# Dilated attention by token parity, and new keys turned by VectorE and stored in 128-byte pieces

## The reference

```
h = rms(x); z = h @ w_in        # q, k, v of three dilated groups (4 heads of 64 each), q, k, v of a fourth mixer, two gates
for (window, dil) in ((128, 1), (512, 4), (2048, 16)):
    query t attends to keys t, t-dil, t-2*dil, ... not further back than window
    softmax of scores + mask; o_g = p @ v; lse_g = log of the softmax denominator
A = sum over the three groups of o_g, weighted by softmax of lse_g      # for the 256 prompt tokens and for the sample tokens
B = sliding-window attention with sinks
x = x + (sigmoid(g_A) * (A @ w_a) + sigmoid(g_B) * (B @ w_b)) @ w_out
outputs beside y: for every group the last `window` rows of keys and values,
   new_a1/a2/a3/b_prompt (.., tokens, 2, heads, 64) and new_.._sample (.., 8 sequences, tokens, 2, heads, 64)
```

## Time and profile before

| | |
|---|---|
| median of 3 runs | 1465.62 us (1464.95 to 1465.94) |
| profiled execution, its own time | 1465.52 us |
| its span, first to last instruction | 1463.7 us |
| granted clock of TensorE, mean | 0.997 of full |
| busy: TensorE, VectorE, ScalarE, GpSimd | 99%, 54%, 46%, 24% |
| DMA, mean over the span | 239 GB/s, 70.7% of the 16 engines' time |

### The profile page before, as it was taken

The page is one execution under the profiler, slowest core; times in us unless marked ns, Lnnn a source line. Parts: engine busy times, 40 slices in busy tenths (PEclk is TensorE's granted clock), DMA queues, the critical chain, the costliest instruction groups (busy, mean ns, idle before and its releaser), DMA issues.

```text
span 1463.7 us, 30875 instructions
## 1 busy us (share of the span) xinstructions
PE 1451.5 (99%) x11336; PEld 1413.1 (97%) x11336; DVE 794.4 (54%) x1281; ACT 669.2 (46%) x1109; POOL 349.3 (24%) x349
## 2 busy tenths in 40 slices
PE   9999999999999999999999999999999999999997
PEld 9999999999889999999999999999998899999997
DVE  5555445855545755554455554477555476555443
ACT  6444344454554544434444443445555545444442
POOL 1322212212115232220032221132121163222200
PEclk9999999999999999999999999999999999999998
DMA  8985566898764788546788846669878558884563
GB/s 309 357 287 178 167 204 203 314 335 288 247 242 137 257 327 291 181 144 198 220 314 295 293 148 182 203 199 341 297 255 284 181 185 286 315 285 144 161 195 109
DMA packets 94978, 349.79 MB, mean 239 GB/s; under 512 B 12336, under 2 KB 23984, under 8 KB 92208
## 3 DMA queue, kind: packets, MB, share of 16 engines
q1 hardware_dynamic: 94752, 348.64, 70.7%
q10 hardware_dynamic: 144, 0.03, 0.0%
HBM read 343.51 MB, written 94.37 MB: 299 GB/s over the span
## 4 chain that ended last, share of the span: by engine, by line
PE 94%; POOL 2%; DVE 1%; issue 1%; ACT 1%; DMA 1%; SPq 0%; DVEq 0%; ACTq 0%; POOLq 0%
PE ps L643 29%; PE ps L644 28%; PE ps L645 28%; PE ps L891 2%; PE ps L905 2%; POOL ma L1592 1%; PE ps L742 1%; PE ps L829 1%; PE ps L791 1%; POOL mlo L1595 0%; ACT whi L1032 0%; PE ps L752 0%; PE ps L818 0%; PE ps L796 0%; DMA x<-in_x 0%
## 5 line engine op out<-in xcount | busy, mean ns | idle before, releaser
L1254 DVE TENSOR_TENSOR wlo<-raw,whi 128x1024 fp32r<-128x1024 f32 (+2 forms) x414 | 485.4, 1173 | 375.0 <-ACT whi L1032 374.5
L643 PE MATMUL ps<-xhi,whi 128*128 128x320 f32 x2048 | 641.3, 313 | 0.9 <-DVE wlo L1254 0.5
L645 PE MATMUL ps<-xhi,wlo 128*128 128x320 f32 x2048 | 632.7, 309 | 0.0
L644 PE MATMUL ps<-xlo,whi 128*128 128x320 f32 x2048 | 632.6, 309 | 0.0
L1032 ACT ACTIVATE whi<-raw 128x1024 fp32r<-128x1024 f32 (+2 forms) x414 | 397.7, 963 | 307.0 <-PE ps L645 300.7
L643 PEld LDWEIGHTS ps<-xhi,whi 128*128 128x128 f32 x2048 | 384.5, 188 | 11.7 <-issue 9.6
L644 PEld LDWEIGHTS ps<-xlo,whi 128*128 128x128 f32 x2048 | 384.7, 188 | 0.5
L645 PEld LDWEIGHTS ps<-xhi,wlo 128*128 128x128 f32 x2048 | 384.4, 188 | 0.0
L643 PE MATMUL ps<-act_hi,whi 128*128 128x320 f32 x704 | 217.5, 309 | 0.0
L644 PE MATMUL ps<-act_lo,whi 128*128 128x320 f32 x704 | 217.5, 309 | 0.0
L645 PE MATMUL ps<-act_hi,wlo 128*128 128x320 f32 x704 | 217.5, 309 | 0.0
(11 more groups left out here) (157 smaller groups left out, 1185.3 us busy)
## 6 DMA issues: line engine op xcount, KB each, us to landing
out_new_a_sample<-in_cache_a SPq DMA_DIRECT2D x128, 510.0 KB, 5.3
raw<-in_ffn_gate SPq DMA_DIRECT2D x87, 512.0 KB, 3.7
raw<-in_ffn_up SPq DMA_DIRECT2D x87, 512.0 KB, 4.5
raw<-in_w_in SPq DMA_DIRECT2D x80, 512.0 KB, 4.9
kvc<-in_kcache SPq DMA_DIRECT2D x52, 512.0 KB, 6.9
kvc<-in_vcache SPq DMA_DIRECT2D x52, 512.0 KB, 5.3
raw<-in_ffn_down SPq DMA_DIRECT2D x64, 384.0 KB, 3.2
raw<-in_ffn_down SPq DMA_DIRECT2D x64, 320.0 KB, 3.1
```

Source lines behind the costliest of these rows:

```text
L643: pe.matmul(out, w0, hi, start=first, stop=False)
L644: pe.matmul(out, w0, lo, start=False, stop=False)
L645: return pe.matmul(out, w1, hi, start=False, stop=last)
L1254: nc.vector.tensor_tensor(wlo[:, (base + s) % RING, 0:tiles * P], raw[:, (base + s) % RAW, 0:tiles * P], whi[:, (base + s) % RING, 0:tiles ...
```

## The change

Prompt queries and keys of the dilated groups are taken by parity in place of by halves. An item of the dilated attention is now head pair by parity t. It has four blocks of 128 queries by 128 keys: same-parity keys of all three groups, and other-parity keys of group 1. It is done in one part. The S beats of an item hold 8 score matmuls, T 8 transposes, O 8 value products. The operands are read with a step of two elements. The tables of beats and tiles are rewritten. The values of the three groups are laid in `vtok` by parity, still with TensorE transposes.

The new keys are no longer turned by TensorE and copied by ScalarE. A step D, two units behind a key unit, has VectorE transpose `qk` to `kst` in square blocks of 32 x 32. So `kst[32q + r, 32t + f]` holds feature 32q + f of token 32t + r. The store of a key unit is then, for each of the four q, one DMA of prompt rows and two of sample rows, in pieces of 32 floats (128 bytes): 12 DMAs in place of 2. ScalarE no longer has the key stores' semaphore before it; VectorE has it instead, from the fourth key unit on.

```diff
+KEYS_LATER = 2
...
-BEATS = {10: "S0", 12: "T0 S1a", 13: "S1b", 15: "T1a O0", 16: "T1b S2", 18: "T2 O1 S3a", 19: "S3b",
-         21: "T3a O2", 22: "T3b S4", 23: "O3", 24: "T4 S5", 26: "T5 O4 S6", 28: "T6 O5 S7", 30: "T7 O6 S8",
-         32: "T8 O7 S9", 34: "T9 O8 S10", 36: "T10 O9", 38: "O10"}
...
+BLOCKS = (((0, 0), (0, 1), (1, 0), (2, 0)), ((1, 1), (2, 1), (0, 0), (0, 1)))
+NBK = 4
...
+    return slice(parity, SEQ, 2)
...
+BEATS = {10: "S0", 12: "T0 S1", 15: "T1 O0 S2", 18: "T2 O1 S3", 21: "T3 O2 S4", 24: "T4 O3 S5",
+         26: "T5 O4 S6", 28: "T6 O5 S7", 30: "T7 O6 S8", 32: "T8 O7 S9", 34: "T9 O8 S10", 36: "T10 O9", 38: "O10"}
+TILES = {10: 4, 12: 4, 15: 5, 18: 5, 21: 4, 23: 4, 26: 4, 28: 4, 30: 5, 32: 4, 34: 4, 36: 5}
...
-        if u - ROWS_LATER in KV_UNITS:
+        if u - ROWS_LATER in V_UNITS:
             steps.append(("R", u - ROWS_LATER))
             INNER_ROWS[u] = u - ROWS_LATER
         steps.append(("U", u))
...
+        if u - KEYS_LATER in K_UNITS:
+            steps.append(("D", u - KEYS_LATER))
...
+    for n, (t, (g, kp)) in enumerate([(0, _b) for _b in BLOCKS[0]] + [(1, _b) for _b in BLOCKS[1][2:]]):
+        win, dil = DILS[g]
+        gap = (2 * np.arange(P) + t)[:, None] - (2 * np.arange(P) + kp)[None, :]
+        ok = (gap >= 0) & (gap <= win) & (gap % dil == 0)
+        c[:, C_MA + n * P:C_MA + (n + 1) * P] = np.where(ok, 0, NEG)
...
-            kst = sb("kst", [P, KST, 3 * P], F32, att)
...
+            kst = sb("kst", [P, KST, TOK], F32, att)
...
+                return o[:, c, tokens(t)], ps[:, BK_O, 0:P]
...
+                    sp.wait_ge(kturn_done, L * 7 + nk + 1)
+                    src, done = kst[:, nk % KST, :].rearrange("p (t f) -> p t f", f=BLK), kst_out[nk % KST]
+                    t0 = P // BLK if skips_first_rows(KV_UNITS[n]) else 0
+                    dst = prompt.rearrange("l n (t p) v h d -> l p (n t) v (h d)", p=BLK)
+                    for q in range(P // BLK):
+                        rows, f0 = slice(BLK * q, BLK * (q + 1)), heads + BLK * q
+                        to = dst[at(L), :, :, kv, f0:f0 + BLK].rearrange("l p t f -> (l p) t f")
+                        sp.dma_start(to, src[rows, t0:SEQ // BLK, :]).then_inc(done, 16)
+                        for half in range(2):
+                            to = sample[at(L), 4 * half:4 * half + 4, :, kv, f0:f0 + BLK].rearrange(
+                                "l b t f -> (l b) t f")
+                            sp.dma_start(to, src[rows, SEQ // BLK + half, :]).then_inc(done, 16)
+                    return
...
+                    if g == 0:
+                        src = vtok[P // 2:P, :, cols]
+                    dst = prompt.rearrange("l n (p t) v h d -> l p (n t) v (h d)", t=2)
...
+                        for n, (g, kp) in enumerate(BLOCKS[t]):
...
-                                               qk[r, qk_slot("q", g, c), t * P:(t + 1) * P],
-                                               qk[r, qk_slot("k", g, c), part * P:(part + 1) * P],
+                                mm = pe.matmul(ps[:, BK_S + j, n * P:(n + 1) * P],
+                                               qk[r, qk_slot("q", g, c), tokens(t)],
...
+                        for n in range(2 * NBK):
...
+                        for m, (g, kp) in enumerate(BLOCKS[t]):
...
+                                mm = pe.matmul(ps[HD * j:HD * (j + 1), BK_O, 0:P], vtok[:, kp, f0:f0 + HD],
+                                               pts[:, n * P:(n + 1) * P], start=m == 0, stop=m == NBK - 1)
...
-                    if not skips_first_rows(u):
-                        pe.transpose(ps[:, BK_ROWS, 0:P], src[:, 0:P], ident)
-                    pe.transpose(ps[:, BK_ROWS, P:2 * P], src[:, P:2 * P], ident)
-                    if COLS[u][0] == "k":
-                        pe.transpose(ps[0:NB * NT, BK_ROWS, 2 * P:3 * P], src[:, SEQ:TOK], ident)\
-                            .then_inc(kvt_done, 1)
-                        return
...
+                    by_parity = COLS[u][1] < NG
+                    pe.transpose(ps[:, BK_ROWS, 0:P], src[:, tokens(0) if by_parity else slice(0, P)], ident)
+                    pe.transpose(ps[:, BK_ROWS, P:2 * P], src[:, tokens(1) if by_parity else slice(P, SEQ)], ident)
...
-                            nc.scalar.activation(to[:, t0:2 * P], ps[:, BK_ROWS, t0:2 * P], ACT.Copy)
-                            nc.scalar.activation(new, ps[0:NB * NT, BK_ROWS, 2 * P:3 * P], ACT.Copy)\
-                                .then_inc(kvtok_done, 1)
...
+                    elif kind == "D":
+                        nk = K_UNITS.index(n)
+                        dve.wait_ge(rope_done, L * 17 + QK_UNITS.index(n) + 1)
+                        if nk >= KST:
+                            dve.wait_ge(kst_out[nk % KST], (L * k_stores(nk % KST) + nk // KST) * 192)
+                        t0 = P if skips_first_rows(n) else 0
+                        nc.vector.transpose(kst[:, nk % KST, t0:TOK], qk[:, qk_slot(*COLS[n]), t0:TOK])\
+                            .then_inc(kturn_done, 1)
...
-                        if parts(i) == 2:
-                            mm.then_inc(s_part, 1)
-                        if part < parts(i) - 1:
-                            continue
-                        if parts(i) == 2:
-                            dve.wait_ge(s_part, (L * len(TWO_PARTS) + TWO_PARTS.index(i)) * 2 + 2)
-                            mm = nc.vector.tensor_tensor(mx[:, 0:2], mx[:, 0:2], mx[:, 2:4], ALU.max)
```

More of the change, by code:

```diff
@@ L136, in mixer_steps @@
             else:
-                steps.append((word[0], (i, part)))
-                if word[0] == "S" and part == parts(i) - 1:
+                steps.append((word[0], i))
+                if word[0] == "S":
                     norm.append(("N", i))
@@ L164 @@
 OUT_ORDER = [n for _k, n in STEPS if _k == "W"]
-S_EVENTS = [n for _k, n in STEPS if _k == "S" and ITEMS[n[0]][0] != "SA"]
+S_EVENTS = [n for _k, n in STEPS if _k == "S" and ITEMS[n][0] != "SA"]
 T_EVENTS = [n for _k, n in STEPS if _k == "T"]
@@ L412, in segments, with segment @@
             kind, _, t = ITEMS[i]
[L413 to L422, removed]
+            return {"B": (P * (t + 1), 4), "A": (NBK * P, 2), "SB": (N_SB, 4), "SA": (N_SA, 1)}[kind]
+        def segment(i, s):
+            w = segments(i)[0]
+            return e[:, s * w:(s + 1) * w]
         def out_place(i, o):
@@ L543, in store_kv @@
                 heads = P * c
-                sp.wait_ge(kvtok_done, L * 14 + n + 1)
+                prompt, sample = a[f"new_{name}_prompt"], a[f"new_{name}_sample"]
+                w = sample.shape[2]
+                sample = sample[:, :, w - NT:w, :, :, :].rearrange("l b t v h d -> l b t v (h d)")
                 if kind == "k":
                     nk = K_UNITS.index(KV_UNITS[n])
-                    src, done = kst[:, nk % KST, 0:2 * P].rearrange("p (t f) -> p t f", t=2), kst_out[nk % KST]
-                    parts = [(slice(0, NB), kst[0:NB * NT, nk % KST, 2 * P:3 * P])]
-                else:
-                    cols = slice(v_slot(g, c) * P, (v_slot(g, c) + 1) * P)
-                    src, done = vtok[:, :, cols], v_out
-                    parts = [(slice(4 * half, 4 * half + 4), new_rows(g, c)[:, half, :]) for half in range(2)]
@@ L564, in mixer_loads @@
+                sp.dma_start(dst[at(L), :, :, kv, heads:heads + P].rearrange("l p t f -> (l p) t f"), src)\
+                    .then_inc(v_out, 16)
+                for half in range(2):
+                    to = sample[at(L), 4 * half:4 * half + 4, :, kv, heads:heads + P].rearrange("l b t f -> (l b) t f")
+                    sp.dma_start(to, new_rows(g, c)[:, half, :]).then_inc(v_out, 16)
             def mixer_loads(L):
@@ L822, in values @@
                     elif kind == "A":
[L823 to L831, removed]
+                        pe.wait_ge(kvtok_done, L * 7 + (3, 6)[c])
+                        for m, (g, kp) in enumerate(BLOCKS[t]):
+                            for j in range(2):
+                                n = j * NBK + m
+                                f0 = v_slot(g, c) * P + HD * j
+                                mm = pe.matmul(ps[HD * j:HD * (j + 1), BK_O, 0:P], vtok[:, kp, f0:f0 + HD],
+                                               pts[:, n * P:(n + 1) * P], start=m == 0, stop=m == NBK - 1)
                         mm.then_inc(s_pv, 1)
@@ L951, in mixer_products @@
                         mm.then_inc(unit_used, 1)
-                    elif kind == "S" and ITEMS[n[0]][0] != "SA":
-                        scores(*n)
+                    elif kind == "S" and ITEMS[n][0] != "SA":
+                        scores(n)
                     elif kind == "T":
-                        transposes(*n)
+                        transposes(n)
                     elif kind == "O":
@@ L1182, in mixer_act @@
                         else:
-                            if part == 0 and users:
+                            if users:
```

131 lines of the change are left out of this document (51 added, 80 removed).

## The result

The changed kernel takes 1491.1 us (median of 4 runs, 1487.8 to 1492.8) against 1465.8 for the one before beside it: ratio 1.017, 95% interval 1.016 to 1.018. That is 25.3 us slower, where 11.6 were forecast; it also lies 3 us above the forecast's own range of 1468.5 to 1488 for this cause. The profiled execution took 1491.44 us, its span is 1489.6.

What follows compares the result with a forecast made beforehand. TensorE, 99% busy, was taken to bound the kernel. Per layer, 10.4 us of waits behind SyncE's key stores less 4.6 saved gives 5.8, twice 11.6: 1465.5 + 11.6 = 1477.1 us, own range 1468.5 to 1488, overall 1455 to 1504.

Steps and rivals of the forecast that it cites:

- the mechanism: SyncE's queue in the mixer: key stores delay cache tiles, TensorE waits 10.4 us per layer; chance 0.45.
- the forecast's own subtraction: Tile 25's end, 367.5 us, minus 357.1 without waits gives TensorE's wait per layer, 10.4 us.
- the savings: TensorE's stream: fewer key transposes, shorter dilated beats and fewer interruptions save 4.6 us per layer, 9.3 in all.
- the operands in steps: TensorE operands read two floats apart: taken as free; upper bound, each such matmul doubling, adds 5.9 us per layer.
- the queue's walk: SyncE's issues from the load at place 17 to tile 23's: 74.2 us (low 69.7), from 286.4 to 360.6.
- the low bound: Prompt stores of 32 rows in SyncE's queue: 0.48 us each at the low bound, 0.67 taken.
- it lands after the least time seen, 3.4 us: Cache tile 23's load: with only small stores ahead, lands 3.4 us after its issue at 360.6 us.
- The two further loads: After tile 23 lands: two more loads of 512 KB at 397 GB/s take 2.6 us.
- Tile 25's own products: TensorE's products on the last key tile take 0.9 us, ending at 367.5 us.
- Nearly cancelled: Rival: prompt stores issue at the low 0.48 us, net loss 1.3 us per layer, 1468.1 us; chance 0.08.
- The queue keeps up: Rival: small stores issue at 0.59 us or less, never waiting below about 0.53; 1456.2 us; chance 0.27.
- Pieces of 128 bytes bind the DMA engines: Rival: small pieces bind from 50 ns each; 1502 us at 80 ns, 1544 at 130; chance 0.20.

Runs made afterwards that it cites:

- run 1: Changed kernel with all key stores issued from place 30 on, behind the last key tile, and seven `kst` buffers in place of three: 1456.8 us, ratio to before 0.994.
- run 2: Changed kernel without the eight sample stores of each key unit, their outputs missing: 1456.3 us, ratio to the kernel before 0.994.
- run 3: Changed kernel without the four prompt stores of each key unit, their outputs missing: 1461.2 us, ratio to the kernel before 0.9975.
- run 5: Kernel before with 12 key stores per unit, each sample store covering two sequences by 64 values in 256-byte pieces: 1483.8 us, ratio 1.0122.
- run 6: Changed kernel's parity and tables alone, with keys turned by TensorE, copied by ScalarE and stored as in the kernel before: 1460.3 us, ratio to before 0.9966.
- run 4: Kernel before with its key stores cut into 12 DMAs per unit, pieces left at 512 bytes, sample stores of 8 rows: 1465.9 us, ratio 1.0004.
- run 7: Changed kernel with 18 extra matmuls, results unused, on TensorE ahead of key tile 23: 1487.2 us, ratio to the kernel before 1.0148.

## Why the forecast had the right cause and less than half the size

**Right: the mechanism.** The forecast put the loss in SyncE's queue, behind the key stores, at tiles 23 to 25, released by DMAs of `kvc`. That is what the waits, the chain and the queue show, and runs 1, 2 and 3 confirm it (run 5 confirms the queue, at another tile). TensorE stops before L909 (L891 before), for 9.9 us in layer 0 between 285 and 385 us (90.11 of 100 busy), where a wait of 10.4 was forecast. That the two agree is luck: with the end of tile 25 as measured, 372.2 us, the forecast's own subtraction gives 372.2 - 357.1 = 15.1 us. Idle time is only part of such a delay. Work at half clock counts as busy, and so does the tail of products that stand alone (0.65 us for a tile's 16, against 0.48 in the earlier trace rows).

**Nearly right: the savings.** Forecast 9.3 us for both layers: 5.3 by the parity and 4.0 by the key transposes. Measured 5.0 (run 6) and 3.5 (run 6 against run 1), 8.5 in all.

**Right: the operands in steps cost nothing.** The scores' group in the kernel before (L742), then two groups of the changed kernel, shapes apart:

```profile
L742 PE MATMUL ps<-qk 64*128 64x128 f32 x144 | 11.3, 289 | 0.0
L763 PE MATMUL ps<-qk 64*128 64x128 f32 x128 | 9.7, 289 | 0.0
L848 PE MATMUL ps<-pts,vtok 128*64 128x128 f32 x128 | 8.8, 279 | 0.0
```

Scores (L763) take 289 ns each as before, when they read their operands without a step, and run 6 came out at 1460.3 us where steps that cost anything near the upper bound would have given 1468 or more. The value transposes stay 0.11 us apart. The rule of the Trainium skill (SBUF — State Buffer, Door 1: The DMA port swizzle), that a step is free while two accesses still fall into one 16-byte line, agrees with these numbers. VectorE's transpose takes 0.50 us for 128 x 320 (0.53 taken) and 0.37 for 128 x 192.

**Right in sum, wrong in parts: the queue's walk.** From the load at place 17, at 285.94, to tile 23 at 361.78 are 75.8 us, against 74.2 forecast. By the timeline of the queue with 0.04 us of gap for each issue, the six key units took 45.2 us (forecast 48.7: the prompt stores issue in 0.45 us, the low bound, not in the 0.62 that was chosen; the sample stores in 0.61, as 0.64 was expected). But the 12 weight loads took 0.59 each, not 0.38, the 18 tiles 0.52, not 0.46, and the stores of a value unit 2.05, not 1.84. These errors nearly cancel, and that they do is luck.

**Wrong: the terms after the issue, and one that was not there.** The steps that failed are the landing of tile 23, taken at the least time seen, and the clock, whose cost the sum doesn't have. For layer 0, tile 25 was to end at 367.5 and ended at 372.2 us:

- Issue of tile 23: 361.8 for 360.6, +1.2 us.
- *"it lands after the least time seen, 3.4 us"*: it took some 5.7 us, to 367.5, when TensorE starts on it: +2.3. The forecast had only small stores ahead of it; but within 2.6 us the queue issued a weight load, the three last key tiles and a value tile, and the DMA engines are busy for 0.99 of the time from 366 us on. That these loads slowed each other is the likely reason and not shown. What the runs do show is that the least time was no fair choice, late queue or not. The landings of `kvc` from 285 to 366 us in the changed kernel and in run 5 (both late, run 5 without pieces of 128 bytes), and in run 1, where no key tile is late, against 3.4/6.1/9.5 in the earlier trace rows:

```profile
DMA to landing us min/median/max: 4.5/7.7/10.1
DMA to landing us min/median/max: 4.8/7.0/9.7
DMA to landing us min/median/max: 3.5/6.7/10.0
```

- The two further loads took 3.0 us, not 2.6: +0.4.
- Tile 25's own products took 1.7 us, not 0.9, at a clock of 0.50: +0.8.
- The clock's term was missing. After 372.2 us the weight products go at 0.267 us for another twelve steps, 12 x 0.12 = +1.4 us.

With 0.4 us that the savings fell short of, that is 6.5 us; layer 0 lost 12.1 in place of 5.8, which is 6.3 more. So of what was missed per layer about two fifths is the landing (2.7), a third the clock (2.2), and the rest is small. The earlier stretch of low clock, at 318 us, doesn't count in this sum: it only makes TensorE come later to tiles 23 to 25, for which it waits anyway. Layer 1, which the forecast took as a copy, lost 13.6; TensorE stands still there for 11.8 us (88.18 of 100 busy from 1018 us) where it is 9.9 in layer 0, and its longest wait for a key tile is 6.0 us where layer 0's is 4.1. Why that tile came later still was not followed up.

**The rivals.** *Nearly cancelled* gave 1468.1 us, and its condition was met, as the prompt stores issue at the low bound. That the time was far above it is owed to the terms named above. *The queue keeps up* gave 1456.2 us, and that is what runs 1 and 2 measured (1456.8 and 1456.3), but the change as it stands doesn't meet its condition: 0.59 us or less for a store with its gap, where 45.2 / 72 = 0.63 were measured. The forecast also had TensorE never wait below 0.53, which is 6.4 us per key unit; in run 3 it waits 2.4 us in all at 5.2. The limit was set too high, for the reasons above: longer landings, longer issues of the other loads. *Pieces of 128 bytes bind the DMA engines* is refuted by runs 1 and 2. What they cost at most can be read where hardly anything else moves, from 300 to 304 us in the changed kernel (the DMA view of that stretch):

```profile
DMA packets 930, 0.17 MB, mean 43 GB/s; under 512 B 915, under 2 KB 915, under 8 KB 929
...
q1 hardware_dynamic: 929, 0.17, 21.9%
```

0.219 x 16 engines x 4 us over 929 packets is 15 ns each, below the 21 taken and far from the 50 or so at which it would bind. The sign that the prediction gave for this rival, landings of 10 us or more, was badly chosen: one took 10.1 us, but before it was 9.5, and 9.7 in run 5, without any such piece.

**Left open.** Why a store of 32 rows takes 0.61 us to issue when it covers four sequences, and one of 8 rows 0.30, while a prompt store takes 0.45, the runs don't show: runs 4 and 5 only show that the shape decides and not the bytes, as all these sample stores carry 4 KB. Key stores issued from another engine's queue weren't tried.

## What to carry to other kernels

A DMA's price in the issuing queue depends on its shape and is paid in order, so before splitting a store, sum up issue times between it and the next load that somebody waits for; if the sum doesn't fit, put the stores behind the loads (here 34 us for three changed lines and four more buffers). When forecasting a wait for a late load, don't take the best landing time seen, and add what TensorE loses after it by its lower clock. Average slack in a queue (95.8 us of waits in the earlier trace rows) says little about a stretch in which everything comes at once.

## What the runs showed of the hardware

- Small stores from one queue differ by a factor of two in the time to issue them, whatever their bytes: 0.61 us for 32 rows over four sequences, 0.61 for 16 rows over two, 0.30 for 8 rows of one, 0.45 for 32 partitions with 4 or 8 pieces each (medians of 96, 96, 96 and 48).
- TensorE's clock fell from 2.4 to 1.2 GHz around its waits. After a stop of 4.13 us at 363.36 the granted clock was 0.50 from 366 us, and full speed was back only at about 376 us, after 5.3 us of products without a stop, the last 3.6 of them weight products; in layer 1, after a stop of 6.04 us, it was back 1.8 us after the first weight product. At 318 us it fell after stops of only 1.58 and 0.73 us, and in run 7, with stops of much the same length there (1.5 and 0.7), it stayed at 1.00. In run 7 it also fell at 366 us with small products in the gap, 128 x 128 by 32 columns and no stop.
- Some 15,900 more packets below 512 bytes (28192, before 12336) cost nothing that can be measured: 1456.8 us with all of them in run 1, 1456.3 in run 2 with some 4,000 fewer.
